# Weight rings at byte remainders 256 and 384 modulo 512 in a two-block transformer kernel

## What is computed

```python
# first block
x = x + 0.5 * swiglu(rms_norm(x, norm_ffn1_w), ffn1_w_in, ffn1_w_out)      # 1024 -> 2*2816 -> 1024
x = x + hybrid_mixer(rms_norm(x, norm_mix_w), ...)                         # state-space scan + attention
x = x + memory_cross_attention(rms_norm(x, norm_cross_w), rms_norm(mem, norm_mem_w), ...)
x = x + 0.5 * swiglu(rms_norm(x, norm_ffn2_w), ffn2_w_in, ffn2_w_out)
x = rms_norm(x, norm_final_w)
# second block
proj = rms_norm(x, g_pre_mix) @ w_in                                       # 1024 -> 5120
mixed = (gate_attn * (attention @ w_attn_out) + gate_conv * (conv @ w_conv_out)) @ w_o
x = x + rms_norm(mixed, g_post_mix)
f = square(relu(rms_norm(x, g_pre_mlp) @ w_up)) @ w_down                   # 1024 -> 4096 -> 1024
x = x + rms_norm(f, g_post_mlp)
x = x + sigmoid(rms_norm(x, g_ple) @ w_ple_gate) * (p @ w_ple_proj)
```

## The kernel before

| tile | before | change |
|---|---|---|
| `w_raw` | 0 | 0 |
| `w_hi` | 0 | 256 |
| `w_lo` | 0 | 384 |
| `gx_hi`, `gx_lo`, and the high and low parts named ff, ys, o, ox, cv, o2, up, p | 0 | 0 |
| `m_hi`, `m_lo` (memory of the cross-attention) | 64 | 64 |
| `wdt_hi`, chunk k of 16 columns | 448 + 64k | 448 + 64k |
| `wdt_lo`, chunk k | 192 + 64k | 64 + 64k |
| `consts` (the transposes' identity) | 0 | 384 |
| `rstd_row`, `sumsq`, `square`, `rfin_row` | 192 | 64 |

## Time and profile before

### The profile page before, as it was taken

How to read it: one execution, slowest core, us unless ns; L and a number is a source line. 1 busy time by engine, 2 the same in 40 slices (tenths; PEclk the granted TensorE clock), 3 DMA queues, 4 the chain that set the end, 5 groups by cost and what they waited for, 6 DMA issues and landing times.

```text
span 2133.4 us, 29164 instructions
## 1 busy us (share of the span) xinstructions
PE 2114.8 (99%) x10122; PEld 1740.7 (82%) x10122; DVE 829.8 (39%) x1489; ACT 803.6 (38%) x1345; POOL 1120.5 (53%) x1493
## 2 busy tenths in 40 slices
PE   9999999999999999999999999999999999999999
PEld 7888888878887778877888888887787888888887
DVE  5222211762841766143322222208744474023244
ACT  5222232325834655323322223326554343122233
POOL 6555555673354337725655555554545466555554
PEclk9999999999999999999999999999999999999999
DMA  6322233233322213412332223321222223332322
GB/s 214 119 98 98 99 106 106 85 99 96 114 99 79 75 55 122 155 40 89 99 98 98 95 94 117 99 96 63 79 89 79 89 80 108 99 99 99 99 89 80
DMA packets 61344, 207.71 MB, mean 97 GB/s; under 512 B 6616, under 2 KB 8088, under 8 KB 61256
## 3 DMA queue, kind: packets, MB, share of 16 engines
q1 hardware_dynamic: 55216, 195.84, 27.8%
q10 hardware_dynamic: 6040, 10.65, 1.5%
HBM read 204.31 MB, written 4.77 MB: 98 GB/s over the span
## 4 chain that ended last, share of the span: by engine, by line
PE 42%; issue 28%; POOL 27%; DVE 2%; POOLq 0%; ACT 0%; DMA 0%; SPq 0%; DVEq 0%; ACTq 0%
POOL w_lo L463 27%; PE bank L516 11%; PE bank L518 11%; PE bank L517 11%; PE bank L678 1%; PE bank L680 1%; PE bank L679 1%; PE bank L908 1%; PE bank L932 1%; PE bank L840 1%; PE bank L920 0%; DVE gx_lo L2394 0%; DVE bank L2403 0%; PE bank L846 0%; DVE x L2405 0%
## 5 line engine op out<-in xcount | busy, mean ns | idle before, releaser
L463 POOL TENSOR_TENSOR w_lo<-w_raw,w_hi 128x256 fp32r<-128x256 f32 x1448 | 1087.1, 783 | 933.4 <-ACT w_hi L1283 933.3
L516 PE MATMUL bank<-gx_hi,w_hi 128*128 128x512 f32 (+1 forms) x1768 | 674.9, 382 | 7.8 <-DVE gx_lo L2394 4.5
L518 PE MATMUL bank<-gx_hi,w_lo 128*128 128x512 f32 (+1 forms) x1768 | 668.1, 378 | 0.0
L517 PE MATMUL bank<-gx_lo,w_hi 128*128 128x512 f32 (+1 forms) x1768 | 667.6, 378 | 0.0
L1283 ACT CAST w_hi<-w_raw 128x1024 fp32r<-128x1024 f32 x364 | 378.4, 1045 | 347.9 <-PE bank L518 291.8
L516 PEld LDWEIGHTS bank<-gx_hi,w_hi 128*128 128x128 f32 x1768 | 332.6, 188 | 74.2 <-DVE gx_lo L2394 6.4
L518 PEld LDWEIGHTS bank<-gx_hi,w_lo 128*128 128x128 f32 x1768 | 332.5, 188 | 62.1
L517 PEld LDWEIGHTS bank<-gx_lo,w_hi 128*128 128x128 f32 x1768 | 332.7, 188 | 60.5 <-issue 0.2
L516 PE MATMUL bank<-ff_hi,w_hi 128*128 128x512 f32 x352 | 136.9, 389 | 0.0
L517 PE MATMUL bank<-ff_lo,w_hi 128*128 128x512 f32 x352 | 136.9, 389 | 0.0
L518 PE MATMUL bank<-ff_hi,w_lo 128*128 128x512 f32 x352 | 136.9, 389 | 0.0
(11 more groups left out here) (358 smaller groups left out, 2703.4 us busy)
## 6 DMA issues: line engine op xcount, KB each, us to landing
w_raw<-wstream SPq DMA_DIRECT2D x364, 512.0 KB, 3.5
bias_spread<-bias_rows ACTq DMA_DIRECT2D x1, 2560.0 KB
square<-cum_rows ACTq DMA_DIRECT2D x8, 256.0 KB, 3.5
rfin_row<-cum_rows ACTq DMA_DIRECT2D x8, 256.0 KB, 3.1
outT<-ple_o SPq DMA_DIRECT2D x8, 256.0 KB, 2.0
x<-xT SPq DMA_DIRECT2D x3, 512.0 KB, 8.0
square<-bias_spread ACTq DMA_DIRECT2D x4, 256.0 KB, 2.6
rfin_row<-bias_spread ACTq DMA_DIRECT2D x4, 256.0 KB, 2.7
```

Of the source, the lines that this page charges most:

```text
L463: ins = nc.gpsimd.tensor_tensor(w_lo[:, s, part], w_raw[:, s, part], w_hi[:, s, part].bitcast(F32), ALU.subtract)
L516: nc.tensor.matmul(dst, hi, rhs[0], start=first, stop=False)
L517: nc.tensor.matmul(dst, hi, rhs[1], start=False, stop=False)
L518: return nc.tensor.matmul(dst, lo, rhs[0], start=False, stop=last)
```

## The change

The code gets a table of shifts. `w_raw` is put on a multiple of 2048, the ring of high parts starts 256 bytes further than it otherwise would, the ring of low parts 384 bytes past a multiple of 512. The shift of each activation is 0. In the shared region each 8 KB of offset gets 512 bytes more (`GAP`), so the places of tiles in it move by multiples of 512 and the region starts on a multiple of 2048. The scratch that is reserved for DMA descriptors goes from 16384 to 1024 bytes to make room. No instruction is added, removed or reordered: without line numbers, every engine's sequence of instructions is the same before and with the change.

```diff
+GAP = 512
+SHIFT = {"gx": 0, "ff": 0, "ys": 0, "o": 0, "ox": 0, "cv": 0, "o2": 0, "up": 0, "w_hi": 256, "w_lo": 384}
...
-        cursor[0] = -(-cursor[0] // LINE) * LINE
+        cursor[0] = -(-cursor[0] // LINE) * LINE + SHIFT["gx"]
...
+        cursor[0] = -(-cursor[0] // LINE) * LINE
         w_raw = fixed("w_raw", [RING, UNIT])
+        cursor[0] += SHIFT["w_hi"]
         w_hi = fixed("w_hi", [RING, UNIT], F32R)
+        cursor[0] += SHIFT["w_lo"] - SHIFT["w_hi"]
         w_lo = fixed("w_lo", [RING, UNIT], F32R)
...
-        REGION = -(-cursor[0] // 512) * 512
-        cursor[0] = REGION + 96 * 1024 + 64
+        REGION = -(-cursor[0] // LINE) * LINE
+        cursor[0] = REGION + 96 * 1024 + 12 * GAP + 512
...
-        def at(name, kb, shape, dt=F32):
-            off = REGION + int(kb * 1024)
+        def at(name, kb, shape, dt=F32, shift=0):
+            off = REGION + int(kb * 1024) + int(kb // 8) * GAP + shift
...
-        ff_hi = at("ff_hi", 0, [FC, S], F32R)
-        ff_lo = at("ff_lo", 44, [FC, S], F32R)
+        ff_hi = at("ff_hi", 0, [FC, S], F32R, shift=SHIFT["ff"])
+        ff_lo = at("ff_lo", 44, [FC, S], F32R, shift=SHIFT["ff"])
...
-    nc = bacc.Bacc("TRN2", target_bir_lowering=False, num_devices=1)
+    nc = bacc.Bacc("TRN2", target_bir_lowering=False, num_devices=1, dynamic_dma_scratch_size=1024)
```

More of the change, by code:

```diff
@@ L257, in build @@
         ysq_tmp = at("ysq_tmp", 69, [GH * SHD])
-        ys_hi = at("ys_hi", 16, [DC, S], F32R)
-        ys_lo = at("ys_lo", 32, [DC, S], F32R)
+        ys_hi = at("ys_hi", 16, [DC, S], F32R, shift=SHIFT["ys"])
+        ys_lo = at("ys_lo", 32, [DC, S], F32R, shift=SHIFT["ys"])
         q_T = at("q_T", 48, [AH, S])
@@ L307, in build @@
         bias_h = [square, rfin_row]
-        o_hi = at("o_hi", 48, [AH, S], F32R)
-        o_lo = at("o_lo", 64, [AH, S], F32R)
+        o_hi = at("o_hi", 48, [AH, S], F32R, shift=SHIFT["o"])
+        o_lo = at("o_lo", 64, [AH, S], F32R, shift=SHIFT["o"])
         load_sq = at("load_sq", 0, [DC, S])
@@ L324, in build @@
         qx_T = at("qx_T", 48, [DC, S])
-        ox_hi = at("ox_hi", 64, [DC, S], F32R)
-        ox_lo = at("ox_lo", 80, [DC, S], F32R)
+        ox_hi = at("ox_hi", 64, [DC, S], F32R, shift=SHIFT["ox"])
+        ox_lo = at("ox_lo", 80, [DC, S], F32R, shift=SHIFT["ox"])
         m_sum = at("m_sum", 40.0625, [ML])
@@ L333, in build @@
         v2_tok = at("v2_tok", 16, [TT, S])
-        cv_hi = at("cv_hi", 24, [4, S], F32R)
-        cv_lo = at("cv_lo", 32, [4, S], F32R)
+        cv_hi = at("cv_hi", 24, [4, S], F32R, shift=SHIFT["cv"])
+        cv_lo = at("cv_lo", 32, [4, S], F32R, shift=SHIFT["cv"])
         gates = at("gates", 40, [16, S])
-        o2_hi = at("o2_hi", 0, [4, S], F32R)
-        o2_lo = at("o2_lo", 8, [4, S], F32R)
+        o2_hi = at("o2_hi", 0, [4, S], F32R, shift=SHIFT["o2"])
+        o2_lo = at("o2_lo", 8, [4, S], F32R, shift=SHIFT["o2"])
         cc_t = at("cc_t", 64, [S])
@@ L366, in build @@
         post_sum = rfin_row
-        up_hi = at("up_hi", 16, [HC, S], F32R)
-        up_lo = at("up_lo", 48, [HC, S], F32R)
+        up_hi = at("up_hi", 16, [HC, S], F32R, shift=SHIFT["up"])
+        up_lo = at("up_lo", 48, [HC, S], F32R, shift=SHIFT["up"])
         f_acc = at("f_acc", 80, [DC, S])
```

## The result

| | before | changed |
|---|---|---|
| time, median | 2134.77 us (2134.08 to 2135.24, 4 runs) | 2163.40 us (2162.95 to 2165.76, 4 runs) |
| ratio to before | | 1.0135, 95% interval 1.0121 to 1.0149 |
| profiled execution | span 2133.4 us | 2163.11 us, span 2161.3 us |

The change makes the kernel 28.6 us, 1.3%, slower. The prediction had 2098 us as its likeliest case and this outcome, in kind, as its third rival. The measured time lies inside its range of 2045 to 2176 us only because the range took in that rival's 2176.

What follows compares the result with a forecast made beforehand. The prediction took TensorE's matmul count times start-to-start distance as the bound. From 2134.65 us it subtracted 36.9 us for the weight triples, all other terms zero, giving 2098 us, with a range of 2045 to 2176 us.

Steps and rivals of the forecast that it cites:

- third rival: Dense stages: the matmul rhythm is lost or settles worse with unequal remainders; about 2180 us, chance 0.26.
- What bounds the kernel: TensorE, busy 99% of the span: number of matmuls times start-to-start distance, with 13.3 ns lost a matmul.
- Addresses matter: TensorE's weight load and moving stream meet in memory; remainders decide the loss, 110 us or 5% of the span at stake.
- Step (a): All 2768 triples with stationary weights at 256 and 384, moving tiles at 0: 13.3 ns less each, 36.9 us less.
- the loss of 6 units leaves room: Dense stages' triples: 6 units of 6.67 ns lost in each, taken as room for a gain of two.
- second rival: The remainders do nothing, as what counts repeats every 64 or 128 bytes or other operands differ; 2134.65 us, chance 0.08.
- Step (b): Token stages z, v, v2 and cv, 576 matmuls with moving weights: zero, between 3.8 us more and 6.9 us less.
- (c): Identity, sums and norm rows, some 300 short plain float32 matmuls, at other remainders: zero, at most 2.0 us either way.
- (d): GpSimd's reads and writes of the weight buffers at new remainders: hidden behind TensorE; it would have to grow by 70%.
- (e): The smaller DMA scratch, with weight traffic at 98 GB/s: taken as zero.
- the settled case: Dense stream settles at cv's 233.3 ns a matmul: 55.4 us more, 2190 us.
- the unsettled one: Dense stream does not settle and runs at 231.7 ns a matmul: 41.7 us more, 2176 us.

Runs made afterwards that it cites:

- e1: Changed kernel with both rings back at remainder 0 and the memory's tiles moved from 64 to 0, wider layout and small scratch kept; 2135.29 us.
- g1: Changed kernel with high ring at 0, low ring at 384, every low moving tile but p's 128 bytes further than the high one; 2163.28 us.
- e4: Changed kernel with both rings at 0 and moving tiles at gx 64, ff 128, up 192, o 320, ox 448, the memory's 256; 2157.66 us.
- f0: Changed kernel with high ring at 256, low ring at 0, gx at 0, ff 32, up 96, o 160, ox 224; 2148.18 us.
- e3: Changed kernel with the high ring at 0 and the low ring kept at 384; 2162.86 us.
- f1: Changed kernel with high ring at 0, low ring at 128, gx 64, ff 192, up 128, o 32, ox 96, the memory's 192; 2166.04 us.
- g2: Changed kernel with both rings at 0 and every low moving tile but p's at 128, the high ones at 0; 2164.61 us.
- g4: Changed kernel, rings at 0, moving tiles (high, low): gx (32, 64), ff (64, 96), up (96, 64), o (0, 96), ox (0, 160), memory's (0, 0); 2166.01 us.

## Why the prediction was wrong

- **What bounds the kernel: right.** Matmuls times their distance, clock and waits untouched. The time moved with that distance.
- **Addresses matter: right**: e1 gave ck and cv the distances of gx when their remainder went from 64 to 0. The placements tried, of the same instructions, differ by up to 7.6 ns a matmul, and in the changed kernel a load too is listed 4 ns longer. That speaks against the two places of the Trainium skill that the prediction quoted: in "SBUF — State Buffer", Who interferes with whom, TensorE never waits on anyone, and by "TensorE: Matmul & The Clock Gate", Part 2, the load of the next weights takes no read bandwidth from the running matmul. That it is the load and the stream of TensorE that meet was not shown directly, since no version without the load was tried; what was shown is that shifting either moves the distance, and that shifting all together does not. In g1 the tile streamed and the tile loaded beside it agree each time, and the loss is there all the same.
- **Step (a), two units of 6.67 ns won a triple, 36.9 us less: this is the step that failed**, in its sign. Two units were lost: 693.3 ns a triple against 680.0. I had bounds of both signs and took the gain, because ck (256 columns, one unit won for 64 bytes) seemed the nearest row. It was the wrong row to lean on. In e4 the same shift of 64 wins 2.2 ns with 256 columns (120.0 to 117.8) and loses 2.2 with 512 (226.7 to 228.9), and in the changed kernel gx wins 0.9 with 256 and loses 4.4 with 512. The sign goes with the width, and nearly nine tenths of the matmuls are 512 wide. The argument that "the loss of 6 units leaves room" had no row at all behind it, while three groups spoke for a loss.
- **The two rings taken together.** The prediction let both move "to different places". Of the two, the high ring's 256 is as good as no move (f0, e3): the pattern repeats every 256 bytes. The second rival named a period of 64 or 128 bytes as its reason; it has 256, so half of the change does nothing and the low ring's 384, which is 128, does everything.
- **Step (b), the token stages, zero: small, as taken**, 1.2 us more. cv left its bad side (233.3 to 231.1), v2 went from 226.7 to 228.9. **Steps (c), (d), (e), zero: right.** For (c) the distances of the attentions, the scan and the transposes in the changed kernel add up to the same within 0.1 us; for (d) GpSimd's instruction has 785 ns against 783, with the rings at 256 and 384; for (e) e1, with the small scratch, has 2135.29 us.
- **The third rival happened**, in a milder form than either of its two. It put the settled case at cv's 233.3 ns and 2190 us and the unsettled one at 231.7 and 2176. What came is a settled rhythm at 231.1, by chance near the average of a stream that has not settled. Its price was 41.7 us where the spans differ by 27.9. The 512-column products of stationary weights cost 29.0 us of the 36.9 that 5.0 ns each would be, since they settled at 4.4 ns more and part of them lie in stretches too short to settle, whose distances were already longer before. The 256-column products gave back 1.6 us instead of costing 4.8. The other groups add 0.5 us. Its reason held for 512 columns: 226.67 ns was the low end of all placements tried, and came only where all four tiles were equal modulo 256.

What stays open: which relations of the four tiles (successive streams, or a tile and its own weights) cost in g1, what chooses between two steady distances, why the sign turns with the width, and why the commonest values (102, 103, 104 and 105 times 2.22 ns) are so evenly spaced.

## What to carry to other kernels

In a stream of float32r matmuls with a weight load each, put weights and 512-column moving tiles, high and low parts alike, at the same byte remainder modulo 256 within a partition; a single tile of the four that stands out cost 2 to 3% of the stream in nearly all cases here (231.0 to 233.3 ns against 226.7, in one stage 228.9; the high ring was never the one that stood out). Read the distance from start to start over tens of matmuls, not the listed durations, and look whether it is the same in every stretch. Before leaning on a row for the sign of an effect, check that its shape is the shape of most of the work: here 256 and 512 columns go opposite ways.

## What was unexpected

- The same line of code with the same tiles and remainders ran at 228.9 ns in one stretch and at 233.3 ns in another of the same execution (f1), each steady for hundreds of matmuls; g2 and g4 show the same.
- The pattern repeats after 256 bytes to 0.1 ns (64 and 320, 192 and 448, 0 and 256 in e4).
- 32 bytes are enough to lose 6.7 ns (f0, ff), and none of the other placements came below the 226.67 ns of equal remainders, though plain float32 matmuls of 512 columns are 429.4 ns apart, which is twice 214.7.
- For 256 columns unequal remainders can be better: 113.3 ns in the changed kernel's ck against 120.0 with equal ones.
